# Half of the second block's modulation sums moved from the experts' down tiles into the first attention branch

## The chip, the cores and the metric

The kernel runs on one core of a Trainium2 chip. Its time is that of one execution on the device in microseconds; the time of a kernel is the median of its runs. Engines are named as the profile names them: PE is TensorE, DVE is VectorE, ACT is ScalarE, POOL is GpSimd, SP is SyncE, which here only issues transfers.

## The reference, cut to what matters

Two transformer blocks follow each other on 512 tokens of width 1024. The first block is modulated by six vectors from `silu(c) @ ada_w + ada_b`, has a mixer with two linear-attention branches (HGRN with 8 heads, then GLA with 4), and a mixture of experts (PEER). The second part (latent attention, an MLP, a state-space mixer, a second MLP) has modulation vectors of its own, made from another `c` vector in the same way:

```python
t_ctx = mixer_inputs(modulate(rmsnorm(xc, ...), mod_c[0], mod_c[1]), w_in, ...)
t_lat = mixer_inputs(modulate(rmsnorm(x, ...), mod[0], mod[1]), w_in, ...)
x = x + mod[2] * mixer_output(t_lat, context_states(t_ctx), rows, *mix_w)
x = x + mod[5] * peer(modulate(rmsnorm(x, norm_ffn_g), mod[3], mod[4]), *peer_w)
```

The second block's modulation is a product of one row of 1024 numbers with a matrix of 12288 columns. It depends on the inputs alone, so its 96 columns of 128 numbers can be made at any time before the second block begins. In the kernel one such column is one "modulation tile": 128 partitions by 1024 numbers of `w_mod`, multiplied by the row and summed along it.

## The kernel before, in words

The program is a chain of phases; each phase is one block with five instruction streams that signal each other through semaphores. Four places matter.

**The first attention branch** (`heads_phase` with `hg` true, tiles named `hgrn_...`) runs from about 57 to 494 us. Each of its 8 heads has five weight tiles (`f0`, `f1`, `q`, `v0`, `g0`; `NW` is 5), so 40 tiles of 512 KB. A tile goes through a ring of four slots (`R` is 4): SP loads it (L512) once POOL has finished the tile four places before it, ACT rounds it to its high part (L764), POOL subtracts to get its low part (L528), and PE multiplies the high and low parts. The streams walk through the iterations `it`; in one iteration PE projects head `H = it` and, between those matmuls, does the attention work of head `h = it - 1`, while the norm of head `g = it - 2` is finished. PE's order is written out by hand in `beside(g, h)`: keys, states, scores of the two directions, and then `outputs(h)` beside the `g0` product, which waits for `state_done` of both directions. DVE's order in an iteration is: `finish(g)` (L1038, L1042), `query_decay(h)` (L1010), `mask(h, 0)` (L1014), `forget(H, 0)` (L949, L950), `gates(h)` (L1033), `states(h, 0)` (L1022, L1024), `forget(H, 1)`, `differences(H, 0)` (L972 to L988: two scans and five subtractions), `mask(h, 1)`, `differences(H, 1)`, `products(H, 0)` (L1000 to L1005), `states(h, 1)`, `products(H, 1)`. `forget(H, r)` waits for ACT's store of the `f0` or `f1` product. ACT takes the exponentials of `differences` (L800 to L804) before `products` can start. In its last two iterations there is no head left to project; PE then makes the next branch's low-rank gates (`next_ranks`), which waits for `gr_lo`, the DVE instruction at L1083.

**The experts' down tiles** (`peer`, from about 1895 to 2473 us) are 128 tiles `n` of the experts' second matrix (`in_peer_v`). For each tile SP loads 512 KB of weights (L1448) and, through `load_pair`, the activations (L1633) and the gates (L1635) of the tile four places ahead. DVE multiplies activation by gate (`weigh`, L2111), makes the weights' low part (`low`, L2121) and the activations' low part (`act_low`, L2116); PE has 24 matmuls of 128x384 a tile (L1398), which wait for `p_lo` and `v_lo`. Beside them, on three tiles of four (`n % 4`), DVE makes one modulation tile (`Modulation.dot`, L192: one instruction that multiplies and sums along the row, and a short read of the sum) and one `few_add` (L2020), for which POOL fetches 128 rows of 4 KB by an indirect transfer (L1683). POOL also issues the modulation tiles' loads (L1708), each once the tile three places before is summed. One modulation tile of the 96 is left for behind the loop.

**The class `Modulation`** holds the ring of tiles, the row, and the steps: `start_act` (a sigmoid of the row on ACT, L162), `start_mul` (row times sigmoid on POOL, L166), `dot`, and `finish`, which adds the bias on POOL (L204).

**What sets the order** is the hand-written sequence on each engine; nothing is planned at run time. The expert rows and all transfers of the down tiles share the core's 16 DMA engines.

```python
for n in range(2, V_TILES):
    weigh(n)
    low(n)
    act_low(n)
    if n % 4 and m < M.tiles:
        M.dot(dve, m)
```

## Time and profile before

| what | value |
|---|---|
| median of 3 runs | 3714.02 us (3703.05 to 3714.7) |
| the profiled execution | 3709.89 us |
| its span | 3707.9 us |
| PE busy | 3422.5 us, 92% |
| DVE busy | 2415.1 us, 65% |
| ACT busy | 1508.0 us, 41% |
| POOL busy | 1163.8 us, 31% |
| first attention branch, 110 to 410 us: PE busy | 296.76 of 300 us |
| experts' down tiles, 1900 to 2460 us: PE busy | 542.54 of 560 us |

The profiled execution's own time is 2.0 us over its span. Shares of the whole span say which engine is busiest on average; which wait ends last has to be read in each stage. PE being busy means that its queue was at work, not that it ran at its peak.

### The profile page before, as it was taken

To read this page: it belongs to the slowest core of one execution; us is meant where nothing else is said; L and a number is where in the kernel's file an instruction comes from. 1 tells how busy PE (TensorE), PEld (TensorE's weight loads), DVE (VectorE), ACT (ScalarE), POOL (GpSimd) and SP (SyncE) were. 2 spreads that over 40 slices of the span, in tenths; PEclk is the share of its full clock that TensorE was granted. 3 is DMA by queue.
4 is the path that set the end of the run, shared out by engine and by line. 5 is a ranking of instruction groups with operands and counts; after the bars stand their busy time and mean duration, and the time that the engine had idled before them with its cause. 6 is when DMAs were issued, how large, how long until landed. Compare 5 with 4: busy or idle time off the path is not lost. (4 is left out here: it accounts for less than half of the span.)

```text
span 3707.9 us, 46749 instructions
## 1 busy us (share of the span) xinstructions
PE 3422.5 (92%) x17940; PEld 3005.4 (81%) x17940; DVE 2415.1 (65%) x4052; ACT 1508.0 (41%) x2046; POOL 1163.8 (31%) x797
## 2 busy tenths in 40 slices
PE   7999999979989999689979999989899998699998
PEld 6888877768889999679979999977688887678886
DVE  6655544444557999668858888876564576756354
ACT  5555555445343333345523333345442234434222
POOL 1222222127137888444432332320110024320002
PEclk9999999989999999889989999999999999899999
DMA  5111111036338889556699999961223222222331
GB/s 186 55 52 52 37 52 46 29 113 218 130 93 273 304 305 315 193 217 226 248 359 381 380 379 380 379 240 32 63 92 102 93 90 55 50 87 91 97 97 63
DMA packets 263277, 616.56 MB, mean 166 GB/s; under 512 B 93424, under 2 KB 135664, under 8 KB 260880
## 3 DMA queue, kind: packets, MB, share of 16 engines
q1 hardware_dynamic: 203968, 383.72, 31.6%
q0 software_dynamic: 55584, 202.40, 14.6%
q10 hardware_dynamic: 3504, 27.46, 1.9%
q8 instruction: 143, 2.34, 0.3%
q14 instruction: 78, 0.64, 0.0%
HBM read 556.08 MB, written 52.43 MB: 164 GB/s over the span
## 5 line engine op out<-in xcount | busy, mean ns | idle before, releaser
L1398 PE MATMUL peer_banks<-peer_h_parts,peer_w_parts 128*128 128x384 f32 (+1 forms) x3456 | 650.9, 346 | 25.7 <-POOL peer_w_parts L1688 20.4
L1398 PEld LDWEIGHTS peer_banks<-peer_h_parts,peer_w_parts 128*128 128x128 f32 x3456 | 609.4, 190 | 53.1 <-POOL peer_w_parts L1688 31.4
L1398 PE MATMUL peer_banks<-peer_act_parts,peer_w_parts 128*128 128x384 f32 x3072 | 559.9, 340 | 39.2 <-DVE peer_act_parts L2116 38.6
L1398 PEld LDWEIGHTS peer_banks<-peer_act_parts,peer_w_parts 128*128 128x128 f32 x3072 | 536.5, 190 | 60.8 <-DVE peer_w_parts L2121 43.1
L1398 PE MATMUL ffn_ps<-h_parts,ffn_w_parts 128*128 128x512 f32 x1920 | 441.4, 392 | 18.2 <-DVE h_parts L2734 11.0
L1398 PEld LDWEIGHTS ffn_ps<-h_parts,ffn_w_parts 128*128 128x128 f32 x1920 | 363.2, 189 | 95.1 <-DVE ffn_w_parts L2572 15.7
L1398 PE MATMUL ffn_ps<-ffn_hidden,ffn_w_parts 128*128 128x512 f32 x1920 | 438.1, 390 | 1.5 <-DVE ffn_hidden L2641 1.5
L1688 POOL TENSOR_TENSOR peer_w_parts<-slots,peer_w_parts 128x1024 fp32r<-128x1024 f32 x142 | 351.9, 2479 | 274.8 <-ACT peer_w_parts L1851 272.6
L1398 PEld LDWEIGHTS ffn_ps<-ffn_hidden,ffn_w_parts 128*128 128x128 f32 x1920 | 360.4, 188 | 77.7 <-issue 3.1
L1851 ACT ACTIVATE peer_w_parts<-slots 128x1024 fp32r<-128x1024 f32 x272 | 287.5, 1057 | 208.9 <-PE peer_banks L1398 191.1
L2418 ACT ACTIVATE ffn_w_parts<-slots 128x1024 fp32r<-128x1024 f32 x160 | 168.6, 1057 | 310.8 <-PE ffn_ps L1398 303.5
L2572 DVE TENSOR_TENSOR ffn_w_parts<-slots,ffn_w_parts 128x1024 fp32r<-128x1024 f32 x160 | 197.5, 1239 | 141.8 <-ACT ffn_w_parts L2418 141.5
L1398 PE MATMUL heads_proj_ps<-h_parts,hgrn_w_parts 128*128 128x512 f32 x960 | 269.1, 412 | 9.2 <-DVE hgrn_w_parts L1054 8.6
L1865 ACT ACTIVATE h<-peer_banks 128x384 f32<-128x384 f32 x128 | 63.2, 494 | 350.1 <-PE peer_banks L1398 335.5
L1398 PEld LDWEIGHTS heads_proj_ps<-h_parts,hgrn_w_parts 128*128 128x128 f32 x960 | 168.0, 190 | 39.8 <-DVE hgrn_w_parts L1054 8.7
L2385 POOL TENSOR_TENSOR ffn_total<-x 128x512 f32<-128x512 f32 x4 | 5.5, 1380 | 607.0 <-DVE x L2588 607.0
L528 POOL TENSOR_TENSOR hgrn_w_parts<-x,hgrn_w_parts 128x1024 fp32r<-128x1024 f32 x38 | 96.2, 2532 | 290.8 <-ACT hgrn_w_parts L764 290.8
L1398 PE MATMUL heads_proj_ps<-h_parts,gla_w_parts 128*128 128x512 f32 x576 | 166.3, 426 | 9.0 <-POOL gla_w_parts L528 5.1
L1683 POOL DMA_INDIRECT peer_few_rows<-in_peer_v,peer_few_idx x128 | 156.7, 1224 | 39.6 <-issue 31.3
L1708 POOL DMA_DIRECT2D peer_slab<-in_w_mod x93 | 51.9, 558 | 364.5 <-DVE peer_slab L192 352.4
L2121 DVE TENSOR_TENSOR peer_w_parts<-slots,peer_w_parts 128x1024 fp32r<-128x1024 f32 x128 | 156.1, 1220 | 11.3 <-ACT peer_w_parts L1851 11.1
L1772 PE MATMUL peer_banks<-peer_cols,h 128*128 128x128 f32 x768 | 106.9, 300 | 54.2 <-issue 40.1
(585 smaller groups left out, 5853.0 us busy)
## 6 DMA issues: line engine op xcount, KB each, us to landing
slots<-in_peer_u SPq DMA_DIRECT2D x128, 512.0 KB, 4.2
slots<-in_peer_v SPq DMA_DIRECT2D x128, 512.0 KB, 12.5
slots<-in_mlp_w SPq DMA_DIRECT2D x128, 512.0 KB, 3.5
peer_slab<-in_w_mod POOLq DMA_DIRECT2D x96, 512.0 KB, 7.2
peer_acts<-h SPq DMA_DIRECT2D x128, 192.0 KB, 5.1
peer_gates<-peer_slab ACTq DMA_DIRECT2D x16, 1536.0 KB, 13.5
peer_slab<-peer_acts SPq DMA_DIRECT2D x128, 192.0 KB, 11.8
peer_slab<-peer_gates SPq DMA_DIRECT2D x128, 192.0 KB, 11.2
```

What stands on the lines that cost most here:

```text
L528: nc.gpsimd.tensor_tensor(wp[:, m % 2, 1, :], ring[m % R], wp[:, m % 2, 0, :].bitcast(F32), ALU.subtract).then_inc(w_lo, 1)
L1398: last = nc.tensor.matmul(out, w(a, k), x(b, k), start=start and k == ks[0] and n == 0, stop=stop and k == ks[-1] and n == 2)
L1683: nc.gpsimd.indirect_dma_start(few_slot(CALLS + c), None, v_rows, bass.IndirectOffsetOnAxis(ap=few_idx[:, h, j:j + 1], axis=0)).then_inc(f ...
L1688: nc.gpsimd.tensor_tensor(wp[:, p % 2, 1, :], ring.raw[:, p % R, :], wp[:, p % 2, 0, :].bitcast(F32), ALU.subtract).then_inc(w_lo, 1)
L1708: g.dma_start(M.ring[:, i % MG, :], d["w_mod"][i + 48 + MG]).then_inc(M.ready[i % MG], 16)
L1772: last = nc.tensor.matmul(g_ps[:, b * 1024 + t * P:b * 1024 + (t + 1) * P], rows[:, b, t, :], cols[:, b, t, :], start=True, stop=True)
L1851: A(wp[:, p % 2, 0, :], ring.raw[:, p % R, :], ACT.Copy).then_inc(w_hi, 1)
L1865: A(stage[:, n % 4, :], a_ps[:, n % 2 * T:n % 2 * T + DENSE], ACT.Gelu).then_inc(gelu_done, 1)
L2121: V.tensor_tensor(wp[:, p % 2, 1, :], ring.raw[:, p % R, :], wp[:, p % 2, 0, :].bitcast(F32), ALU.subtract).then_inc(v_lo, 1)
L2385: st.then(G.tensor_tensor(total[:], K.x[:, 0, :], K.x[:, 1, :], ALU.add))
L2418: A(wp[:, m % 4, 0, :], raw[:, m % R, :], ACT.Copy).then_inc(w_hi, 1)
L2572: V.tensor_tensor(wp[:, m % 4, 1, :], raw[:, m % R, :], wp[:, m % 4, 0, :].bitcast(F32), ALU.subtract).then_inc(w_lo, 1)
```

## The change

Of the 96 modulation tiles, 48 (`MOD2_FIRST`) are now summed by DVE in the first attention branch, six in each head (`mod_dots(0)`, `mod_dots(1)`, `mod_dots(2)`, two tiles each), in the iterations that have an `h`. They use a new ring of two slots (`mod_ring`) whose second slot first holds the sigmoid. SP issues their loads: the row and tile 48 at the phase's start, tile 49 at the weight tile `m = 8`, and then `refill(i)` behind the loads of the weight tiles `f0`, `f1` and `q` of the head after next; each refill waits for two sums and issues two tiles of 512 KB. The refills of the last two heads stand at the end of SP's stream. ACT has one more sigmoid and POOL one more multiplication in the first head, and POOL adds the bias at the end. In the experts' down tiles the other 48 are summed on two tiles of four (`n % 8` of 1, 2, 3 and 5), and POOL's loop that issues their loads is written out in the order of the tiles.

```diff
@@ -437,6 +437,9 @@
     return m
 
 
+MOD2_FIRST = 48
+
+
 def heads_phase(nc, K, d, name, w_dram, heads, vt, gate_norm, y, scan_scale, lora=False, early=None, nxt=None):
 
 
@@ -459,6 +462,9 @@
         M_ = early if early is not None else heads_memory(ph, hg, vt)
         R = 4 if hg else 3
         if hg:
+            ph.sb("mod_gap", [P, 1280])
+            mod_ring = ph.sb("mod_ring", [P, 2, D])
+            MM = Modulation(nc, K, ph, d, 48, MOD2_FIRST, 2, [(2, 48)], ring=mod_ring, prod=mod_ring[:, 1:2, :])
             ring4 = K.x[:].rearrange("p (r a) t -> p r (a t)", r=R)
             ring = [ring4[:, s, :] for s in range(R)]
         else:
@@ -506,10 +512,25 @@
 
         @block.sync
         def _(sp):
+            def refill(i):
+
+                for n in (2 * i, 2 * i + 1):
+                    if n + 2 < MM.tiles:
+                        sp.wait_ge(MM.multiplied, n + 1)
+                        sp.dma_start(MM.ring[:, n % 2, :], d["w_mod"][48 + n + 2]).then_inc(MM.ready[n % 2], 16)
+
+            if hg:
+                sp.dma_start(MM.rows[:, 0, :], d["c_rows"][2].partition_broadcast(P)).then_inc(MM.rows_in, 16)
+                sp.dma_start(MM.ring[:, 0, :], d["w_mod"][48]).then_inc(MM.ready[0], 16)
             for m in range(R if hg else 2, heads * NW):
                 if m >= R:
                     sp.wait_ge(w_lo, m - R + 1)
                 sp.dma_start(ring[m % R], w_dram[m]).then_inc(ready[m % R], 16)
+                if hg and m == 8:
+                    sp.wait_ge(MM.silu, 1)
+                    sp.dma_start(MM.ring[:, 1, :], d["w_mod"][49]).then_inc(MM.ready[1], 16)
+                if hg and m >= 2 * NW and m % NW < 3:
+                    refill(3 * (m // NW - 2) + m % NW)
             if nxt is not None:
                 sp.wait_ge(nxt.zeroed, 1)
                 sp.dma_start(nxt.wgr[:].rearrange("p (k m) -> p k m", k=KT), d["w_gr"].rearrange("(k p) m -> p k m", p=P)).then_inc(nxt.gr_in, 16)
@@ -518,12 +539,16 @@
                 sp.wait_ge(h_lo, 2 * KT)
                 for m in range(2):
                     sp.dma_start(nxt.ring[:, m, :], d["w_gla"][m]).then_inc(nxt.ready[m], 16)
+                for i in range(3 * (heads - 2), 3 * heads):
+                    refill(i)
 
         @block.gpsimd
         def _(g):
             if nxt is not None:
                 nc.gpsimd.memset(nxt.gw[:], 0.0).then_inc(nxt.zeroed, 1)
             for m in range(2, heads * NW):
+                if hg and m == 6:
+                    MM.start_mul(g, nc.gpsimd)
                 g.wait_ge(w_hi, m + 1)
                 nc.gpsimd.tensor_tensor(wp[:, m % 2, 1, :], ring[m % R], wp[:, m % 2, 0, :].bitcast(F32),
                                         ALU.subtract).then_inc(w_lo, 1)
@@ -532,6 +557,7 @@
                     g.wait_ge(nxt.w_hi, m + 1)
                     nc.gpsimd.tensor_tensor(nxt.wp[:, m, 1, :], nxt.ring[:, m, :], nxt.wp[:, m, 0, :].bitcast(F32),
                                             ALU.subtract).then_inc(nxt.w_lo, 1)
+                MM.finish(g, nc.gpsimd, MM.multiplied)
 
         @block.tensor
         def _(pe):
@@ -888,6 +914,8 @@
                         gates(h)
                     if H is not None:
                         forget(H, 1)
+                        if H == 0:
+                            MM.start_act(act)
                         log_forget(H, 0)
                         log_forget(H, 1)
                         if H:
@@ -1063,11 +1091,18 @@
                         first_low(n)
                     dve.wait_ge(h_hi, n + 1)
                     V.tensor_tensor(dst[:, 1, k, :], src[:, k, :], dst[:, 0, k, :].bitcast(F32), ALU.subtract).then_inc(h_lo, 1)
+            def mod_dots(i):
+
+                for n in (6 * h + 2 * i, 6 * h + 2 * i + 1):
+                    MM.dot(dve, n)
+
             st.then(V.memset(score[:], 0.0))
             for it in range(heads + 2):
                 H = it if it < heads else None
                 h = it - 1 if 0 < it <= heads else None
                 g = it - 2 if it >= 2 else None
+                if hg and h is not None:
+                    mod_dots(0)
                 if lora and H is not None:
                     low_rank(H, 0)
                 if g is not None:
@@ -1078,6 +1113,8 @@
                     query_decay(h)
                     mask(h, 0)
                 if hg:
+                    if h is not None:
+                        mod_dots(1)
                     if h == heads - 1:
                         dve.wait_ge(nxt.gr_hi, 1)
                         V.tensor_tensor(nxt.wgp[:, 1, :], nxt.wgr[:], nxt.wgp[:, 0, :].bitcast(F32), ALU.subtract).then_inc(nxt.gr_lo, 1)
@@ -1086,6 +1123,7 @@
                     if h is not None:
                         gates(h)
                         states(h, 0)
+                        mod_dots(2)
                     if H is not None:
                         forget(H, 1)
                         differences(H, 0)
@@ -1544,7 +1582,8 @@
         gate_in_sb = flat[:, quarter // 2:quarter].rearrange("p (s b t) -> p s b t", s=4, b=TT)
         wact = flat[:, quarter:quarter + 2 * DENSE].rearrange("p (s t) -> p s t", s=2)
         MG = 3
-        M = Modulation(nc, K, ph, d, 48, 4 * 24, MG, [(2, 48)],
+        FIRST = 48 + MOD2_FIRST
+        M = Modulation(nc, K, ph, d, FIRST, 4 * 24 - MOD2_FIRST, MG, [(2, FIRST)],
                        ring=flat[:, 2 * quarter:2 * quarter + MG * D].rearrange("p (s t) -> p s t", s=MG),
                        rows=flat[:, 3 * quarter:3 * quarter + D].rearrange("p (s t) -> p s t", s=1),
                        prod=flat[:, 3 * quarter + D:3 * quarter + 2 * D].rearrange("p (s t) -> p s t", s=1))
@@ -1700,14 +1739,20 @@
             g.wait_ge(slab_out[3], 16 * TT)
             g.dma_start(M.rows[:, 0, :], d["c_rows"][2].partition_broadcast(P)).then_inc(M.rows_in, 16)
             for s in range(MG):
-                g.dma_start(M.ring[:, s, :], d["w_mod"][48 + s]).then_inc(M.ready[s], 16)
+                g.dma_start(M.ring[:, s, :], d["w_mod"][FIRST + s]).then_inc(M.ready[s], 16)
             M.start_mul(g, nc.gpsimd)
 
-            for i in range(M.tiles - MG):
-                g.wait_ge(M.multiplied, i + 1)
-                g.dma_start(M.ring[:, i % MG, :], d["w_mod"][i + 48 + MG]).then_inc(M.ready[i % MG], 16)
-                if BEFORE + LEAD + i < CALLS:
-                    fetch_down(BEFORE + LEAD + i)
+            m, c = 0, BEFORE
+            for n in range(2, V_TILES):
+                if n % 4 and m < M.tiles and n % 8 < 6:
+                    if m + MG < M.tiles:
+                        g.wait_ge(M.multiplied, m + 1)
+                        g.dma_start(M.ring[:, m % MG, :], d["w_mod"][FIRST + m + MG]).then_inc(M.ready[m % MG], 16)
+                    m += 1
+                if n % 4 and c < CALLS:
+                    if c + LEAD < CALLS:
+                        fetch_down(c + LEAD)
+                    c += 1
             M.finish(g, nc.gpsimd, M.multiplied)
             for k in (0, 2, 4):
                 g.wait_ge(sq_done, k + 2)
@@ -2131,7 +2176,7 @@
                 weigh(n)
                 low(n)
                 act_low(n)
-                if n % 4 and m < M.tiles:
+                if n % 4 and m < M.tiles and n % 8 < 6:
                     M.dot(dve, m)
                     m += 1
                 if n % 4 and c < CALLS:
```

## Rows read from the trace of the kernel before

**Rows 1.** busy times of two stretches (columns: engines, clock, DMA share, GB/s)

```profile
110.00:410.00 300.00, 296.76 (x1741) 251.98 (x1740) 163.69 (x248) 157.80 (x227) 75.50 (x30) 1.00 0.18 56
...
1900.00:2460.00 560.00, 542.54 (x2997) 521.25 (x2996) 479.96 (x653) 197.46 (x249) 167.42 (x183) 0.99 1.04 375
```

**Rows 2.** PE in order of time in the down tiles, idle before in brackets

```profile
2131.80 34.88 PE L1398 MATMUL peer_banks<-peer_act_parts,peer_w_parts 128*128 128x384 f32 x192 [0.82 <-DVE peer_act_parts L2116]
...
2259.00 56.53 PE L1398 MATMUL peer_banks<-peer_act_parts,peer_w_parts 128*128 128x384 f32 x312 [2.43 <-DVE peer_act_parts L2116]
```

**Rows 3.** waits within the down tiles: total us, times, longest

```profile
PE peer_banks L1398 <- DVE peer_act_parts L2116: 16.9, 19, 3.2
```

**Rows 4.** page, part 6: transfers, KB each, median us to landing

```profile
peer_slab<-in_w_mod POOLq DMA_DIRECT2D x96, 512.0 KB, 7.2
...
peer_slab<-peer_gates SPq DMA_DIRECT2D x128, 192.0 KB, 11.2
```

**Rows 5.** windows of 4 us around one such wait

```profile
2256.00:2260.00 4.00, 1.57 (x7) 1.28 (x6) 3.31 (x6) 1.58 (x2) 0.00 (x0) 0.87 1.06 360
2260.00:2264.00 4.00, 4.00 (x18) 4.00 (x18) 4.00 (x5) 0.53 (x1) 1.92 (x2) 0.70 1.07 362
```

**Rows 6.** one line each, durations min/median/max in ns: dot, two-input, one-input instruction

```profile
L192 DVE SCALAR_TENSOR_TENSOR peer_slab<-peer_slab x96: 1214/1219/1226, 1904.9 to 2467.1; 128x1024 f32<-128x1024 f32 x96
...
L955 DVE SCALAR_TENSOR_TENSOR gla_na<-gla_log_gate x8: 957/958/1207, 496.8 to 698.3; 128x768 f32<-128x768 f32 x8
...
L988 DVE TENSOR_SCALAR hgrn_e_kd<-hgrn_cum x16: 339/346/2487, 88.2 to 444.6; 128x256 f32<-128x256 f32 x16
```

**Rows 7.** DVE in order of time, one iteration of the first branch

```profile
208.56 0.75 DVE L1038 SCALAR_TENSOR_TENSOR hgrn_osq<-hgrn_o_ps,vec,hgrn_rstd 128x512 f32<-128x512 f32 x1 [9.54 <-ACT hgrn_rstd L836]
...
217.66 0.68 DVE L949 TENSOR_SCALAR hgrn_log_gate<-hgrn_log_gate,oml,lb 128x768 f32<-128x768 f32 x1 [5.31 <-ACT hgrn_log_gate L774]
...
225.89 0.68 DVE L949 TENSOR_SCALAR hgrn_log_gate<-hgrn_log_gate,oml,lb 128x768 f32<-128x768 f32 x1 [2.81 <-ACT hgrn_log_gate L774]
226.60 0.56 DVE L950 TENSOR_SCALAR hgrn_key<-hgrn_log_gate 128x768 f32<-128x768 f32 x1
228.92 2.13 DVE L972 TENSOR_TENSOR_SCAN hgrn_cum<-segf,hgrn_log_gate 128x512 f32<-128x512 f32 x2 [1.76 <-ACT hgrn_log_gate L785]
...
233.47 0.74 DVE L1014 COPY_PREDICATED hgrn_score<-triu,hgrn_score_ps 128x512 f32<-128x512 uint32 x1
...
235.92 2.71 DVE L980 TENSOR_TENSOR hgrn_e_k<-hgrn_cum 128x512 f32<-128x512 f32 x1
...
240.32 0.69 DVE L1000 TENSOR_TENSOR hgrn_e_k<-hgrn_e_k,hgrn_key 128x512 f32<-128x512 f32 x1
...
243.70 1.11 DVE L1024 SCALAR_TENSOR_TENSOR hgrn_state<-hgrn_state,hgrn_e_last,hgrn_kv_ps 128x128 f32<-128x128 f32 x3
```

**Rows 8.** POOL in order of time, the same iteration

```profile
218.58 2.60 POOL L528 TENSOR_TENSOR hgrn_w_parts<-x,hgrn_w_parts 128x1024 fp32r<-128x1024 f32 x1 [13.39 <-ACT hgrn_w_parts L764]
226.81 2.58 POOL L528 TENSOR_TENSOR hgrn_w_parts<-x,hgrn_w_parts 128x1024 fp32r<-128x1024 f32 x1 [5.63 <-ACT hgrn_w_parts L764]
235.46 2.62 POOL L528 TENSOR_TENSOR hgrn_w_parts<-x,hgrn_w_parts 128x1024 fp32r<-128x1024 f32 x1 [6.07 <-ACT hgrn_w_parts L764]
245.16 2.39 POOL L528 TENSOR_TENSOR hgrn_w_parts<-x,hgrn_w_parts 128x1024 fp32r<-128x1024 f32 x1 [7.07 <-ACT hgrn_w_parts L764]
```

**Rows 9.** PE, the same iteration: the first matmul of the outputs

```profile
245.12 0.39 PE L607 MATMUL hgrn_o_ps<-hgrn_score,hgrn_vtok 128*128 128x128 f32 x2
```

**Rows 10.** loads of the first branch's tiles: time to landing, and four issued together

```profile
DMA to landing us min/median/max: 3.3/3.5/6.1
...
37.78 1.75 SPq L249 DMA_DIRECT2D x<-in_w_hg  x4
```

**Rows 11.** all engines, the branch's last iteration with attention work

```profile
466.60 4.69 PE L1398 MATMUL heads_proj_ps<-h_parts,gla_wgr_parts 128*32 128x512 f32 x12 [1.27 <-DVE gla_wgr_parts L1083]
...
467.20 2.37 POOL L533 TENSOR_TENSOR gla_w_parts<-gla_ring,gla_w_parts 128x1024 fp32r<-128x1024 f32 x1 [24.32 <-ACT gla_w_parts L858]
```

## The prediction

> **What bounds the kernel now.** I read the busy times of the two stretches that the change touches first [rows 1]. In the first attention branch PE works 296.76 of 300 us and DVE 163.69: PE is the bound, and a microsecond is lost only where something makes PE wait. In the experts' down tiles PE works 542.54 of 560 us at a granted clock of 0.99, while the core's DMA engines are busy all the time (a share of 1.04) and move 375 GB/s.
>
> PE's rows in order of time show what a down tile costs [rows 2]: 192 matmuls in 34.88 us are 0.182 us each, 24 of them 4.36 us a tile, 17.4 us for four. The waits between them are 19, together 16.9 us, none longer than 3.2 [rows 3]. They end with DVE's activations, but DVE had been idle itself before them: DVE works 479.96 of 560 us, and what it waits for is the transfer that feeds `weigh`. Counting bytes says the same. Four down tiles need four weight tiles and three modulation tiles of 512 KB, three `few_add` fetches of 128 rows of 4 KB (512 KB each), and four activation and four gate slices of 192 KB [rows 4]: 6656 KB, 6.82 MB, at 375 GB/s 18.2 us, against PE's 17.4. The stage takes about 575 us for 128 tiles, 18.0 for four. So the stage is bound by transfers, by a little.
>
> A wait costs more than itself. Around the one of 2.43 us that ends at 2259.00, the granted clock is 0.87 and then 0.70 in two windows of 4 us [rows 5]: (0.13 + 0.30) x 4 = 1.7 us more.
>
> **The down tiles: what is taken away.** Half of the modulation loads go, and two of every four tiles carry one. Four tiles now move 6144 KB, 6.29 MB, 16.8 us at the same rate, under PE's 17.4. Most of the waits should go. All that there is to gain is 16.9 us of waits and about 1.7 for each of the three long ones, 22 us. A reserve of 0.6 us in four tiles is small, so I take 18; the bounds are 12 (a third of the waits, the short ones above all, stay) and 22. The 48 sums themselves, 1.22 us each by the row of the dot [rows 6], lay in DVE's idle time and give PE nothing. The one sum behind the loop goes too; the residual additions behind it are held by PE's last matmuls, so it is counted at nothing, at most 1.2 us.
>
> The Trainium skill (SBUF — State Buffer, section on rules for kernel authors) says to estimate transfers between HBM and SBUF at some 358 GB/s. This trace goes above it with 375 over 560 us. By that figure the new load of four tiles would take 17.6 us, still just over PE's 17.4, and the gain would be near 12, which is an estimate from the page and changes no term here.
>
> **The attention branch: what is added.** Each head gets six dots. A dot starts the next instruction about 1.2 us later, so a pair is 2.4 us, and DVE has room for it on average. What matters is where each pair stands, and I follow one iteration [rows 7 to 9].
>
> Pair 0 stands ahead of `finish`, where DVE idles 9.54 us. Its tiles were asked for long before. Nothing.
>
> Pair 1 follows `mask(h, 0)`, which ends near 212.3, and has until 217.66; DVE idled 5.31 us there. SP may issue its tiles once POOL has done the tile in front, 218.58 - 13.39 = 205.2. A single 512 KB load lands after 3.5 us, and the four loads issued together from 37.78 landed by 45.2 (the last one issued at 39.1, with the longest time, 6.1) [rows 10]; that is (45.2 - 37.78 - 3.3) / 3 = 1.37 for each further one, about 1.3. Behind the weight tile these two land at 210.0 and 211.3. Nothing either.
>
> Pair 2 is the trouble. It stands between `states(h, 0)`, which ends at 225.89 - 2.81 = 223.1, and `forget(H, 1)`. SP issues its tiles only when POOL has done the next weight tile, 218.58 + 2.60 = 221.2. Behind that iteration's weight load they land at 221.2 + 3.5 + 1.3 = 225.9 and 227.2. So the first dot runs from 225.9 to 227.15, when `forget` should have run.
>
> Now POOL comes in. Many DVE instructions don't run beside POOL's subtraction: L955, with two such inputs, takes 957 ns and once 1207; the one-input L988 takes 346 and once 2487 [rows 6]; and L980 at 235.92 takes 2.71 instead of 0.69, because POOL's tile began at 235.46 and ended at 238.08 [rows 7, 8]. Whoever is first is finished first. POOL asks at 226.81, during the first dot, runs from 227.15 to 229.4 (before, it ran 2.2 us after `forget` let it go), and the second dot follows it: 230.5. `forget` takes 0.71 and 0.56: 231.8. `differences(H, 0)` begins there and not at 229.39, when POOL let its scans go.
>
> The chain from there is DVE without a pause until `state_done`, and that has no slack: the last state ends at 243.70 + 1.11 = 244.81 and PE starts the outputs at 245.12 [rows 7, 9]. Without blocks, `differences(H, 0)` takes about 4.2 us (228.92 to 233.47, less what the scans waited): 236.0. But POOL's next tile asks at 235.46, when the last subtraction is just about to start (231.8 + 3.7 = 235.5). If POOL is first, that subtraction waits for POOL's end at 237.9 and the mask starts at 238.3. Before, mask to last state took 11.34 us, of which 2.02 were L980's block: 9.3 now. `products(H, 0)` stands 6.85 - 2.02 = 4.8 behind the mask, from 243.1 to 246.0, and POOL's fourth tile asks at 245.16, inside it: 2.2 more. The last state ends at 238.3 + 9.3 + 2.2 = 249.8, PE starts near 249.9 and has waited 4.8 us. A gap of that length costs clock as well; I take the 1.7 of the row [rows 5], bounds 0 and 3.4.
>
> This holds for the heads whose refills are paced by weight tiles, `h` of 0 to 5. In the first, POOL's tile comes 0.3 us earlier against the loads, and I give it the smaller stall of the next paragraph, 1.6. For `h` of 6 and 7 the refills stand at the end of SP's stream, wait only for sums and land in time. Five heads at 4.8 + 1.7 and one at 1.6 are 34.1 us.
>
> In the last iteration pair 1 stands ahead of L1083, for which PE waited already before it started the ranks at 466.60 [rows 11]. POOL asks at 467.20, between the two dots: 1.2 + 2.2 + 1.1 = 4.5 us later, all of it on PE. If POOL is not between them it is 2.4. Pair 2 lies there in idle time.
>
> The sigmoid, POOL's multiplication and SP's waits in the first head delay DVE by some 4 us between 99 and 112 us, where nothing on PE waits for it; with that cover gone they would cost those 4 once. POOL's bias addition is under 0.5 us and nobody waits.
>
> **The sum.** 34.1 + 4.5 - 18 = +20.6 us. Against the profiled execution's own 3709.9 (span 3707.9) this is 3730.5. The median shown is 4.1 above that execution and the lowest run 6.8 below it, so I put the median at 3732.
>
> **The rivals.** (a) The last subtraction gets in ahead of POOL: it starts at 235.5 and POOL asks at 235.46, so 0.1 us decides. Then mask and POOL run side by side, the scans wait for POOL (238.0), the products end before 245.16, and the last state comes at 246.6: 1.6 us a head, too short for the clock (behind a wait of 0.82 us 192 matmuls ran at the full rate [rows 2]). 6 x 1.6 + 4.5 - 18 = -3.9: 3706 by the profiled execution, 3710 by the median; not slower. For it speaks how near the two times are, against it that any delay of a landing favours POOL. (b) Between them, the subtraction is late but the products are not hit again: 2.5 and 0.5 for five heads, 15 + 1.6 + 4.5 - 18 = +3: 3717. (c) The pairs are hidden: the tiles land by 224.5, as they would if three loads took no longer than one, and the down tiles give all their 22. Then 4.5 - 22 = -17.5, with a remnant of 0.5 a head -14.5: 3697 to 3700. Against it stand the four loads of [rows 10]. (d) The change doesn't do what it says in the down tiles: the gates' landing, 11.2 us [rows 4], is set by SP's queue and not by the load, and only 6 us come back; with the forecast's stalls 3744.
>
> **How the numbers follow.** Forecast with (d) at its side 0.48, of which (d) is 0.06; (a) 0.24; (b) 0.11; (c) 0.17. About 0.3% (11 us) is what a measurement of this kernel can tell from no change. Slower by more: 0.48. Within it: (a) and (b) with a little of (c), 0.37. Faster by more: 0.15. The forecast's own range is 3724 to 3744. For eight in ten I take from 3700, which leaves out most of (c), to 3743.
>
> **What would show it.** In the changed kernel's trace: PE waits for `hgrn_state` before L607 once in each of heads 0 to 5, several us long, and the outputs of a head come some 5 us later against its `v0` product; the first dot of pair 2 follows a wait for a transfer, the second lasts 3.3 us or more; a second of L1004 or L1005 is longer than 2 us in those heads; the granted clock dips there. L1083 comes 4.5 us later against the mask ahead of it. In the down tiles PE waits fall from 19 to a few, and GB/s to about 350. The prediction is wrong if landings are quicker than 1.3 us for each further tile, if a dot does not yield to POOL, or if PE has other work ahead of the outputs.

## The result and the profile after

The changed kernel takes 3686.47 us (median of 7 runs, 3678.2 to 3696.98), the kernel before 3708.38 (7 runs beside them). The ratio is 0.9937, with a 95% interval of 0.9915 to 0.9959: faster by 0.6%, more than the 0.3% that can be told from no change. The forecast was 3732, in a range from 3700 to 3743: the result lies below the whole range, and the change made the kernel faster where slower was forecast. The span of the profiled execution falls from 3707.9 to 3684.7 us, by 23.2.

Two stretches of the changed kernel answer to [rows 1] (same columns: PE, PEld, DVE, ACT, POOL, clock, DMA share, GB/s).

```profile
110.00:410.00 300.00, 287.24 (x1681) 242.86 (x1681) 210.48 (x309) 151.13 (x216) 72.21 (x28) 1.00 0.32 113
1930.00:2430.00 500.00, 500.00 (x2883) 499.37 (x2883) 417.76 (x544) 182.93 (x241) 131.08 (x132) 1.00 1.03 362
```

The attention branch lost: PE's idle time in 300 us went from 3.24 to 12.76. The down tiles won more than I had thought there was: PE and its weight loads are busy without a gap.

PE's matmuls of the down tiles, first the line's own view (count, durations, first and last start, what ended the idle time), then one stretch in order of time and the waits inside the stage:

```profile
L1436 PE MATMUL peer_banks<-peer_act_parts,peer_w_parts x3072: 331/334/658, 1913.0 to 2450.0; 128*128 128x384 f32 x192
its engine sat idle before it (us, times) until:
  DVE peer_act_parts L2161: 21.7, 1
```

```profile
2109.72 50.60 PE L1436 MATMUL peer_banks<-peer_act_parts,peer_w_parts 128*128 128x384 f32 x291
```

The stage runs from 1913.0 to 2450.0, 537.0 us; before it ran from 1895.2 to 2472.2, 577.0. So it gives 40.0 us. The only wait is the first, ahead of the stage. But the 19 waits of [rows 3] held only 16.9 of the 40. The rest is in the matmuls: 50.60 us for 291 are 0.174 us each, where [rows 2] show 0.182, and that row has no wait inside it either. The first line above says how lateness can hide there: the record of a matmul lasts 334 ns, but the next one starts 174 ns behind it. One that starts up to 0.16 us late still begins inside the record ahead of it and leaves no idle time. In the trace of the kernel before, five of the seven tiles that follow the first in that row of 192 begin 0.32 to 0.35 us behind the last matmul of the tile ahead, instead of 0.17.

The branch gives back 17.8 of them, since the stage begins that much later. The outputs of the heads (PE, first matmul of a head, idle before it in brackets) show where:

```profile
146.11 0.46 PE L633 MATMUL hgrn_o_ps<-hgrn_score,hgrn_vtok 128*128 128x128 f32 x2 [1.29 <-issue]
...
199.91 0.46 PE L633 MATMUL hgrn_o_ps<-hgrn_score,hgrn_vtok 128*128 128x128 f32 x2 [2.34 <-issue]
...
253.62 0.46 PE L633 MATMUL hgrn_o_ps<-hgrn_score,hgrn_vtok 128*128 128x128 f32 x2 [2.25 <-issue]
...
306.48 0.46 PE L633 MATMUL hgrn_o_ps<-hgrn_score,hgrn_vtok 128*128 128x128 f32 x2 [1.37 <-issue]
```

Before, they began at 142.60, 193.91 and 245.12 (the last in [rows 9]), one every 51.2 us. Now the first is 3.5 us late and each of the next five heads adds 2.2 on average (2.6, 2.5, 1.7, 2.6 and 1.6): the seventh head's outputs begin at 464.39 instead of 449.92, 14.5 late. Behind them come the ranks, [rows 11]; here PE and POOL, and the two dots on DVE between which POOL got in:

```profile
485.54 4.18 PE L1436 MATMUL heads_proj_ps<-h_parts,gla_wgr_parts 128*32 128x512 f32 x12 [5.69 <-DVE gla_wgr_parts L1120]
```

```profile
481.71 2.34 POOL L558 TENSOR_TENSOR gla_w_parts<-gla_ring,gla_w_parts 128x1024 fp32r<-128x1024 f32 x1 [24.42 <-ACT gla_w_parts L884]
```

```profile
480.60 1.21 DVE L192 SCALAR_TENSOR_TENSOR hgrn_mod_ring<-hgrn_mod_ring,hgrn_c_rows 128x1024 f32<-128x1024 f32 x1
...
481.74 3.40 DVE L192 SCALAR_TENSOR_TENSOR hgrn_mod_ring<-hgrn_mod_ring,hgrn_c_rows 128x1024 f32<-128x1024 f32 x1
...
485.07 0.41 DVE L1120 TENSOR_TENSOR gla_wgr_parts<-gla_wgr,gla_wgr_parts 128x256 fp32r<-128x256 f32 x1
```

The wait rose from 1.27 to 5.69, by 4.4; the ranks are 18.9 late. The sum is 14.5 + 4.4 - 40.0, with 1.1 won between the ranks and the down tiles and 1.0 behind them: -23.2, the difference of the spans. The 1.1 is less than executions differ by: the kernel before, `half_loads` and `half_sums` (below) have the same code up to the down tiles and reach them at 1895.2, 1894.8 and 1891.4.

### The profile page after: what moved, and what is told of

Same layout as the page of the kernel before. It is cut to its first block and busy times, and to the rows that moved or that the text cites. A ratio compares the mean times of both kernels' runs of the same rounds, so it can differ in the third digit from the quotient of the medians.

```text
span 3684.7 us, 46757 instructions
## 1 busy us (share of the span) xinstructions
PE 3401.0 (92%) x17940; PEld 3002.9 (81%) x17940; DVE 2434.0 (66%) x4052; ACT 1500.3 (41%) x2047; POOL 1131.0 (31%) x751
## 3 DMA queue, kind: packets, MB, share of 16 engines
q8 instruction: 143, 2.34, 0.3%
## 5 line engine op out<-in xcount | busy, mean ns | idle before, releaser
L1436 PE MATMUL peer_banks<-peer_act_parts,peer_w_parts 128*128 128x384 f32 x3072 | 537.3, 336 | 21.7 <-DVE peer_act_parts L2161 21.7
L1436 PE MATMUL ffn_ps<-h_parts,ffn_w_parts 128*128 128x512 f32 x1920 | 442.0, 393 | 18.2 <-DVE h_parts L2779 10.9
L1722 POOL DMA_INDIRECT peer_few_rows<-in_peer_v,peer_few_idx x128 | 148.2, 1158 | 126.5 <-DVE peer_few_acc L2065 97.4
L1817 PEld LDWEIGHTS peer_banks<-peer_cols,h 128*128 128x128 f32 x768 | 102.2, 211 | 58.6 <-issue 58.6
```

The lines of the kernel that those rows point to most:

```text
L1436: last = nc.tensor.matmul(out, w(a, k), x(b, k), start=start and k == ks[0] and n == 0, stop=stop and k == ks[-1] and n == 2)
L1722: nc.gpsimd.indirect_dma_start(few_slot(CALLS + c), None, v_rows, bass.IndirectOffsetOnAxis(ap=few_idx[:, h, j:j + 1], axis=0)).then_inc(f ...
L1817: last = nc.tensor.matmul(g_ps[:, b * 1024 + t * P:b * 1024 + (t + 1) * P], rows[:, b, t, :], cols[:, b, t, :], start=True, stop=True)
```

## The experiments

### What sets the pace of the down tiles

**Each half of the change alone.** `branch_only` has the 48 sums in the branch and still all 96 beside the down tiles, so 48 are made twice:

```diff
-        FIRST = 48 + MOD2_FIRST
-        M = Modulation(nc, K, ph, d, FIRST, 4 * 24 - MOD2_FIRST, MG, [(2, FIRST)],
+        FIRST = 48
+        M = Modulation(nc, K, ph, d, FIRST, 4 * 24, MG, [(2, FIRST)],
...
-                if n % 4 and m < M.tiles and n % 8 < 6:
+                if n % 4 and m < M.tiles:
```

> The changed kernel's 48 sums in the attention branch stay, and the down tiles again do all 96 as before (the first 48 are made twice). Theory of two separate shares: the branch costs its 18.9 us up to the ranks, the down tiles take their 576.6 us again, so about +18 us against before. Rival, that the two halves act on each other (the branch's cost is only seen because of something later): under +8.

Measured: 3725.52 us, ratio 1.0045 (1.0026 to 1.0064). The down tiles run from 1914.5 to 2488.0, 573.5 us. When nothing pays for it the branch costs 17 us by the ratio and 14 by the medians, near the 18 expected and well above the rival's 8.

`down_only` leaves the 48 sums of the branch out, with their loads, the sigmoid and the multiplication (their columns are zero), and has the other 48 on two tiles of four. Of its edits to the changed kernel:

```diff
             def mod_dots(i):
-                for n in (6 * h + 2 * i, 6 * h + 2 * i + 1):
-                    MM.dot(dve, n)
+                return
...
-                MM.finish(g, nc.gpsimd, MM.multiplied)
+                nc.gpsimd.memset(K.mod[:, 48:96], 0.0)
```

> Nothing of the change in the attention branch (its 48 columns are set to zero and never summed); the down tiles as in the changed kernel. Theory of two separate shares: -40 us against before, with the first down matmul at 1895 and PE at 4.16 us a tile. My forecast's step (PE needs 4.36 us a tile, only the waits can go): -18 to -22.

Measured: 3672.81 us, ratio 0.9896 (0.9879 to 0.9912); the stage runs from 1899.2 to 2435.7, 536.5 us. So the gain of 40 us belongs to the down tiles, and the loss to the branch.

**Transfers or VectorE.** Taking a sum away takes two things away, 512 KB of transfer and 1.22 us of DVE. Both kernels here are the kernel before with one of the two halved. `half_loads` makes all 96 sums, every second one over the data that already lie in the ring:

```diff
-                g.dma_start(M.ring[:, i % MG, :], d["w_mod"][i + 48 + MG]).then_inc(M.ready[i % MG], 16)
+                if (i + MG) % 2 == 0:
+                    g.dma_start(M.ring[:, i % MG, :], d["w_mod"][i + 48 + MG]).then_inc(M.ready[i % MG], 16)
```

> The kernel before with all 96 sums in the down tiles, but only every second modulation tile is loaded; the others are summed over what lies in the slot, so their values are not the modulation's. It takes away the transfers and leaves DVE its work. Theory T (transfers set the pace of the down tiles): nearly all of the 40 us come back, stage about 540. Theory V (DVE sets it: its five instructions of a tile with a sum take 4.42 us back to back, against 4.16 of PE): three tiles of four stay at 4.42, the stage stays at 560 or more, gain under 16.

`half_sums` loads all 96 tiles and replaces every second sum by a memset of its one column:

```diff
-                    M.dot(dve, m)
+                    (M.skip if m % 2 else M.dot)(dve, m)
```

> The kernel before with all 96 loads in the down tiles, but every second sum is left out (a one-column memset stands in its place and releases the slot), so half of the second block's modulation is missing. It takes away DVE's work and leaves the transfers. Theory T: 6.82 MB in four tiles at 380 GB/s are 17.9 us, the stage stays near 575 and nothing is gained. Theory V: the stage falls to about 540, -35 us.

Measured: `half_loads` 3668.76 us, ratio 0.9888 (0.9869 to 0.9907), stage 1894.8 to 2431.2, 536.4 us. `half_sums` 3705.6, ratio 0.9987 (0.9977 to 0.9996), stage 1891.4 to 2464.9, 573.5 us. The same stretch of both, `half_loads` first:

```profile
1930.00:2430.00 500.00, 500.00 (x2892) 500.00 (x2890) 463.03 (x634) 189.13 (x244) 153.68 (x130) 1.00 1.01 354
```

```profile
1930.00:2430.00 500.00, 475.66 (x2673) 468.31 (x2672) 386.08 (x544) 172.66 (x222) 153.88 (x168) 0.99 1.05 380
```

With DVE busier than in the kernel before (463 of 500 us, 431 before) and half the modulation loads, PE never starves; with DVE at 386 and all loads, it starves as before. The transfers set the pace, and DVE does not. `half_loads` also frees POOL from issuing half of the loads; that it is the bytes that count rests on the DMA share of 1.05 and on the byte counts below, not on a run of its own.

**How many have to go.** `moved_32` takes the third pair out of each head and leaves 64 sums beside the down tiles, on four of every eight; `moved_16` keeps only the pair at the start of an iteration and leaves 80, on five of every eight. Their edits to the changed kernel, that of `moved_32` first:

```diff
-MOD2_FIRST = 48
+MOD2_FIRST = 32
...
-                if hg and m >= 2 * NW and m % NW < 3:
-                    refill(3 * (m // NW - 2) + m % NW)
+                if hg and m >= 2 * NW and m % NW < 2:
+                    refill(2 * (m // NW - 2) + m % NW)
...
-                for n in (6 * h + 2 * i, 6 * h + 2 * i + 1):
+                for n in (4 * h + 2 * i, 4 * h + 2 * i + 1):
...
-                        mod_dots(2)
...
-                if n % 4 and m < M.tiles and n % 8 < 6:
+                if n % 4 and m < M.tiles and (n % 8 < 6 or n == 6):
```

```diff
-MOD2_FIRST = 48
+MOD2_FIRST = 16
...
-                if hg and m >= 2 * NW and m % NW < 3:
-                    refill(3 * (m // NW - 2) + m % NW)
+                if hg and m >= 2 * NW and m % NW == 0:
+                    refill(m // NW - 2)
...
-                if n % 4 and m < M.tiles and n % 8 < 6:
+                if n % 4 and m < M.tiles and (n % 8 < 7 or n == 7):
```

> 32 sums in the branch, two pairs a head and no third pair; 64 beside the down tiles, on four of every eight tiles as the 48 are in the changed kernel, but up to the stage's end. Theory T (transfers set the pace of the down tiles until their rate is low enough for PE to): the changed kernel's stage moves 355 GB/s x 520 us and 16 tiles more come to 8.4 MB, so 199 MB in the whole stage, which at the 380 GB/s of the kernel before takes 524 us, less than PE's 532: the stage stays at 537 to 541 us. The branch costs 8 to 10 us instead of 18.9. Time about 3677 to 3681. Rival (each sum beside the down tiles costs its share, 40 us / 48 = 0.83 us, whatever the rate): the stage takes 550, and the time is 3690.

> 16 sums in the branch, only the pair at the start of each iteration; 80 beside the down tiles, on five of every eight tiles. Theory T (the down tiles take the longer of PE's time and the bytes at some 380 GB/s): 199 MB of the kernel with 32 moved and 16 tiles more of 0.52 MB are 208 MB, at 380 GB/s 547 us, above PE's 532, so the stage takes 547 to 552 us; the first output is within 2 us of the kernel before, the ranks too; the time about 3681 to 3686, 10 us above the kernel with 32. Rival (even spreading of the sums over the tiles is what counted, or every sum costs its share of 0.83 us): the stage takes 537 to 541 with even spreading and the time 3671, or 564 and the time 3697.

Measured: `moved_32` 3674.1 us, ratio 0.9905 (0.9883 to 0.9926), stage 539.2 us (1897.9 to 2437.1), as the byte count said. In the changed kernel the sums beside the down tiles are used up early (the last begins at 2318.5, and the stage's last quarter carries none); `moved_32` fills that quarter, and the stage grows by only 2.2 us. `moved_16` 3690.55, ratio 0.9955 (0.9939 to 0.9972), stage 555.8 us (1899.3 to 2455.1): above the forecast of 547 to 552 (and of 3681 to 3686 for the time), and below the rival's 564. Its stretch and its waits:

```profile
1930.00:2430.00 500.00, 493.83 (x2773) 478.22 (x2772) 429.41 (x578) 180.88 (x231) 152.88 (x158) 1.00 1.05 379
```

```profile
PE peer_banks L1433 <- DVE peer_act_parts L2158: 27.1, 9, 21.7
```

Of its 27.1 us of waits 21.7 are the first, ahead of the stage, so 5.4 us lie inside, and yet the stage is 18.8 us longer than with 48 moved. Counting bytes gives the rest. Eight down tiles need 10240 KB without modulation and 512 KB for each modulation tile. At the 380 GB/s at which the engines are full (share 1.05) six, five and four tiles per eight make 35.9, 34.5 and 33.1 us, and PE needs 537.0 / 16 = 33.6. The longer of the two, times 16: 574, 552 and 537, against 577.0, 555.8 and 537.0 to 539.2 measured. PE's 33.6 is itself taken from the measured 537.0, so the independent figures are 574 and 552. So the last step of 16 tiles back to 96 costs 21.2 us, 1.33 each, close to the 1.38 us that 512 KB take at that rate; the step from 64 to 48 is worth 2.2 at most.

The Trainium skill (HBM Reference, Specifications) says that a core that streams alone goes well above its share of some 358 GB/s. The trace agrees in that, with 380 GB/s over 500 us; the some 425 that the page gives as measured are not reached here.

### What the branch costs, and why less than forecast

One iteration of the changed kernel, DVE in order of time, is the counterpart of [rows 7]; POOL's rows are those of its subtraction of [rows 8]:

```profile
232.12 1.23 DVE L192 SCALAR_TENSOR_TENSOR hgrn_mod_ring<-hgrn_mod_ring,hgrn_c_rows 128x1024 f32<-128x1024 f32 x1 [3.00 <-DMA hgrn_mod_ring<-in_w_mod]
...
233.38 3.29 DVE L192 SCALAR_TENSOR_TENSOR hgrn_mod_ring<-hgrn_mod_ring,hgrn_c_rows 128x1024 f32<-128x1024 f32 x1
...
241.50 2.55 DVE L1016 TENSOR_SCALAR hgrn_e_kd<-hgrn_cum 128x256 f32<-128x256 f32 x1
...
251.17 0.69 DVE L1033 TENSOR_TENSOR hgrn_e_q<-hgrn_e_q,hgrn_q 128x512 f32<-128x512 f32 x1
...
252.41 1.11 DVE L1052 SCALAR_TENSOR_TENSOR hgrn_state<-hgrn_state,hgrn_e_last,hgrn_kv_ps 128x128 f32<-128x128 f32 x3
```

```profile
232.84 2.74 POOL L553 TENSOR_TENSOR hgrn_w_parts<-x,hgrn_w_parts 128x1024 fp32r<-128x1024 f32 x1 [5.63 <-ACT hgrn_w_parts L790]
241.51 2.39 POOL L553 TENSOR_TENSOR hgrn_w_parts<-x,hgrn_w_parts 128x1024 fp32r<-128x1024 f32 x1 [5.92 <-ACT hgrn_w_parts L790]
251.25 2.83 POOL L553 TENSOR_TENSOR hgrn_w_parts<-x,hgrn_w_parts 128x1024 fp32r<-128x1024 f32 x1 [7.35 <-ACT hgrn_w_parts L790]
```

In this iteration the chain is the one that was forecast up to the mask: the wait for the third pair's transfer, the second dot lengthened beside POOL (3.29), the last subtraction lengthened too (2.55 for 0.35). The products are not: L1033 takes its usual 0.69, and the states end 2.7 us later in the iteration than before, not 5.

In the next head the subtraction is not caught. It begins 0.04 us ahead of POOL, where above it was 0.01:

```profile
295.20 0.35 DVE L1016 TENSOR_SCALAR hgrn_e_kd<-hgrn_cum 128x256 f32<-128x256 f32 x1
```

```profile
295.24 2.56 POOL L553 TENSOR_TENSOR hgrn_w_parts<-x,hgrn_w_parts 128x1024 fp32r<-128x1024 f32 x1 [5.94 <-ACT hgrn_w_parts L790]
```

That is rival (a) of the prediction. Of the six heads with the late transfer, the second, third and fifth are caught and add 2.5 to 2.6 us; the fourth and sixth are not and add 1.6 to 1.7; the first is not either. In `branch_only`, whose branch is the same, four of the six are caught, and not the same ones.

**Is that luck?** L1033 began 0.08 us ahead of POOL's fourth tile. `late_memset` puts a short memset in front:

```diff
                         mod_dots(2)
+                        if H is not None:
+                            nc.vector.memset(gap[:, 0:256], 0.0)
```

> The changed kernel with a memset of 128x256 elements on VectorE, some 0.3 us, behind the third pair in seven heads: no loads, no sums. In the changed kernel the last product of the head ends at 251.86 and POOL's fourth subtraction begins at 251.25, and the products were not lengthened: by my chain they escaped it by less than 0.1 us. Theory E (a knife edge): 0.3 us later the last product is caught and lasts 2.5 us or more, the states' end moves by 2 us a head or more and the time rises by 12 us or more. Rival (the order of the two engines keeps the product clear): the outputs come 0.3 us later each, and the time rises by 2 us.

Measured: 3693.48 us (10 runs, 3686.54 to 3707.75), ratio 0.9966 (0.9953 to 0.9979). The memset takes 0.27 us. The same iteration:

```profile
251.50 0.68 DVE L1033 TENSOR_TENSOR hgrn_e_q<-hgrn_e_q,hgrn_q 128x512 f32<-128x512 f32 x1
```

```profile
251.56 2.85 POOL L553 TENSOR_TENSOR hgrn_w_parts<-x,hgrn_w_parts 128x1024 fp32r<-128x1024 f32 x1 [7.33 <-ACT hgrn_w_parts L790]
```

None of the 12 L1033 between 142 and 455 us was lengthened (mean 681 ns; 684 in the changed kernel). But the memset does not test the edge at the products. This iteration is 0.30 us late before its memset begins (the third pair's first dot is at 232.42, in the changed kernel at 232.12), and the memset's own 0.27 us are absorbed by the last subtraction, which again waits for POOL:

```profile
241.89 2.48 DVE L1016 TENSOR_SCALAR hgrn_e_kd<-hgrn_cum 128x256 f32<-128x256 f32 x1
```

```profile
241.81 2.42 POOL L553 TENSOR_TENSOR hgrn_w_parts<-x,hgrn_w_parts 128x1024 fp32r<-128x1024 f32 x1 [5.93 <-ACT hgrn_w_parts L790]
```

From the end of POOL's third tile on, the two kernels run alike: L1033 begins 7.3 us behind that end, and POOL's fourth tile 9.7 us behind the third's start. POOL's requests do not follow DVE's chain. They come behind ACT's rounding (L790), which stands in ACT's order behind its store of PE's product, and the store had waited for PE (the changed kernel, fourth tile):

```profile
249.36 0.38 ACT L797 ACTIVATE hgrn_v<-heads_proj_ps 128x256 f32<-128x256 f32 x1 [2.81 <-PE heads_proj_ps L1436]
...
250.11 1.06 ACT L790 ACTIVATE hgrn_w_parts<-x 128x1024 fp32r<-128x1024 f32 x1
```

So they keep their place against PE: the fourth tile begins 0.12 us ahead of the moment at which PE starts to wait for the outputs (251.25 against 253.62 - 2.25 = 251.37), and before it began 0.04 us behind the outputs' start [rows 8, 9]. In the 12 heads of the changed kernel, `branch_only` and `late_memset` whose subtraction was caught, L1033 is listed between 0.08 us ahead of POOL's fourth tile and 0.01 behind it, and it took its 0.68 to 0.69 us each time. So it was luck, of a kind that repeats: the products escape by less than 0.1 us in each such head. What they would take 0.2 us later was not tried.

More heads are caught at the subtraction here. L1016 averages 938 ns over 11 in the changed kernel and 1128 here, which with 0.35 and 2.5 us for the two cases is 3 of 11 caught and 4 of 11:

```profile
L1016 DVE TENSOR_SCALAR hgrn_e_kd<-hgrn_cum 128x256 f32<-128x256 f32 x11 | 10.3, 938 | 0.0
```

```profile
L1016 DVE TENSOR_SCALAR hgrn_e_kd<-hgrn_cum 128x256 f32<-128x256 f32 x11 | 12.4, 1128 | 0.0
```

The first head, outside that stretch, is caught here too, so it is three heads against five. The seventh head's outputs begin at 468.19, 3.8 later. Two more caught heads are 1.9 of them, and 1.7 are clock: behind the fifth head's wait of 2.33 us the granted clock was 0.58 from 362 to 366 us, where the changed kernel has 1.00. That leaves some 0.2 us for all seven memsets. The medians differ by 7 us, but they were taken at different times, the runs of both kernels scatter over 19 to 21 us, and the two profiled spans are equal (3684.8 and 3684.7); what the memset costs in all stays open. That the caught heads and the dips of the clock also make these runs scatter, where the four of `early_refill_ranks` (below) lie within 0.9 us, is likely but not shown, since one execution of each kernel is profiled.

**The transfer of the third pair.** `early_refill` asks for it one weight tile earlier, and for the next head's first pair too, which had time either way:

```diff
-                if hg and m >= 2 * NW and m % NW < 3:
-                    refill(3 * (m // NW - 2) + m % NW)
+                if hg and m >= 2 * NW and m % NW < 2:
+                    i = 3 * (m // NW - 2)
+                    for r in ((i, i + 1), (i + 2,))[m % NW]:
+                        refill(r)
```

> The changed kernel with the third pair's loads asked for one weight tile earlier in every head (behind the first tile of the head instead of the second); sums, their places and the down tiles are as they are. Theory B (the branch's loss is the third pair: it waits 3.00 us for its transfer and pushes the states, whose end the outputs wait for): the wait of about 3 us before L192 is gone, the outputs' waits of 1.3 to 2.3 us in heads 2 to 7 are gone, the ranks' matmuls begin near 475 instead of 485.5, and the time falls by about 10 us to 3676. Rival (the second dot of the third pair is caught by another of POOL's subtractions, or the earlier transfers slow the weight tiles): the waits move and stay, and the time falls by 3 us or less.

Measured: 3679.4 us, ratio 0.9912 (0.9891 to 0.9932). The dots of all heads together, in the changed kernel and here (sum, mean ns | idle before and what ended it):

```profile
L192 DVE SCALAR_TENSOR_TENSOR hgrn_mod_ring<-hgrn_mod_ring,hgrn_c_rows 128x1024 f32<-128x1024 f32 x48 | 71.8, 1523 | 20.9 <-DMA hgrn_mod_ring<-in_w_mod 19.4 <-DVE hgrn_e_q L1033 1.3
```

```profile
L192 DVE SCALAR_TENSOR_TENSOR hgrn_mod_ring<-hgrn_mod_ring,hgrn_c_rows 128x1024 f32<-128x1024 f32 x48 | 56.8, 1219 | 2.7 <-DMA hgrn_mod_ring<-in_w_mod 1.4 <-DVE hgrn_e_q L1035 1.3
```

The waits for transfers fall from 19.4 to 1.4 us and no dot is lengthened any more. The outputs of the first seven heads begin every 51.2 us again, with no wait before them, the seventh at 451.71, and the ranks begin at 472.82. The third head's:

```profile
246.92 0.39 PE L635 MATMUL hgrn_o_ps<-hgrn_score,hgrn_vtok 128*128 128x128 f32 x2
```

So the late transfer, with the subtractions that it let collide, was the branch's loss in the middle heads: 12.7 of the 14.5 us. The 7 us between the medians are less than that: the down tiles begin at 1905.6, 7.4 us earlier than in the changed kernel. Most of the 5.3 us in between went in clock. Over the 60 us around the ranks the granted clock is 0.80 here (450 to 510 us) and 0.86 in the changed kernel (460 to 520), which is 3.6 us, and 5.2 are gone by the first matmul of the mixer's output product (815.3 against 822.8).

**The last head.** In two kernels the last head's second pair stands behind the low-rank subtraction:

```diff
-                    if h is not None:
+                    if h is not None and h < heads - 1:
                         mod_dots(1)
                     if h == heads - 1:
                         dve.wait_ge(nxt.gr_hi, 1)
...
+                        mod_dots(1)
```

> As the kernel with 32 moved sums, and in the last head the second pair of sums stands behind the low-rank subtraction instead of ahead of it. If the 4.5 us of the tail are that subtraction made late by the pair (a dot lengthened to 3.40 us by POOL, and the other), the wait of 5.69 us before the ranks' matmuls falls back to about 1.3 and the time falls by another 4 to 4.5 us, to 3673 to 3677. Rival: something else behind it is as late, and the time falls by 1 us or less.

> 48 moved, loads asked for earlier as in the kernel with early refills, and in the last head the second pair behind the low-rank subtraction. The wait of 4.67 us before the ranks' matmuls falls to about 1, the ranks begin near 469, the time falls by some 4 us against early refills alone, to about 3675: the same as the kernel with 32 moved and this order (3672), since both stages of down tiles are at PE's pace. Rival (the pair, moved behind, makes the third pair and the forget gate late, and the last head's outputs with them): the last outputs stay at 491 and the time at 3679.

Measured: `moved_32_ranks` 3672.17 us, ratio 0.9899 (0.9883 to 0.9916), ranks at 467.71; from `moved_32` (470.36, a wait of only 2.08) there was less to win than I had written, and the time fell by 2 us. `early_refill_ranks` 3671.01 us (3670.58 to 3671.49), ratio 0.9902 (0.9886 to 0.9919), ranks with no wait at all:

```profile
468.11 3.76 PE L1439 MATMUL heads_proj_ps<-h_parts,gla_wgr_parts 128*32 128x512 f32 x12
```

Against `early_refill` the time fell by 8 us where some 4 were forecast, more than the wait of 4.67 that is gone: the granted clock from 450 to 510 us is back at 0.89, as in the kernel before, from 0.80. The last outputs begin at 485.15 against 484.56 before: the 48 sums now cost the branch 0.6 us there, and 1.5 at the ranks. Every run of both is below the lowest of the changed kernel (3678.2), and they stand where `down_only` stands, which makes no sums in the branch at all; which of the two is better can't be told.

## Why the prediction was wrong

Two terms of the sum failed, and it took both to leave the range.

**The first step that failed: "All that there is to gain is 16.9 us of waits and about 1.7 for each of the three long ones, 22 us."** The stage gave 40.0, and the sum with 40 in the place of 18 is -1.4, on the other side. I had taken PE's 4.36 us a tile [rows 2] for its floor, because the row shows no wait. But a start that comes up to 0.16 us late leaves no idle time in the row, since each record lasts 334 ns; and the ends of matmuls in this profile are modelled, so that some that are fed late are shown as longer ones (the mean from 1900 to 2460 us is 339 ns, in the changed kernel from 1930 to 2430 it is 334). PE's own pace is 4.19 us a tile (537.0 / 128), 0.175 us a matmul. The transfers' 18.2 us for four tiles, which I had also worked out, should have been set against 16.8 and not 17.4: 1.2 us (by the 18.0 that the stage took) to 1.4 for each four tiles, times 32, is 38 to 45.

The kernel before had the number. In [rows 1] the weight loads (PEld) are busy 521.25 us for 2996, which is 0.174 each, the fed pace, and they leave 38.75 of the 560 us idle, where the matmuls leave 17.46. The reading is rough: in 500 us of `half_sums` they leave 31.7 and in `moved_16` 21.8, for stages that are 36.5 and 18.8 us longer than the fed one. The Trainium skill (Perfetto Trace Analysis, Identifying the Most-Contended Engine) says that the busy share of matmuls is a bad measure of how near TensorE is to its limit and names that of the weight loads instead (beside MFU, the work done as a share of the peak). The traces agree: PEld goes to 499.37 of 500 us in the changed kernel.

**The bound: right.** Transfers set the pace of the stage, by experiment: 536.4 us with half of the modulation loads and 573.5 with half of the sums. That it is "by a little" was wrong in size. Rival (d), gates that land late for SP's sake, fell: the waits for them did not hold the stage once the loads were gone.

**The second step that failed, in the branch: 34.1 us for 14.5, right in kind and more than twice too large.** The first two pairs cost nothing and the third waited for its transfer, 3.00 us. POOL collided with the second dot (3.29 us) in all six heads, as forecast. But "POOL's fourth tile asks at 245.16, inside it: 2.2 more" failed in every head. POOL did ask inside the products, at 251.25 in an iteration that PE reached 6.0 us later than before; the product then at work was the last of the five, had begun 0.08 us earlier, and was finished first. And the collision with the last subtraction, on which "0.1 us decides", came in some heads and not in others, where I had let it come in all five. The caught heads added 2.5 to 2.6 us, rival (b)'s 2.5; the others of the five 1.6 to 1.7, rival (a)'s 1.6. The first head cost 3.5 us and not 1.6, of which 1.29 is its wait before the outputs.

The clock term of 1.7 a head has the right size and the wrong count. In the changed kernel the granted clock stayed at 1.00 through all these waits. In `branch_only`, with the same branch, it fell behind two of the six, those of 2.27 us before 252.93 and of 2.26 us before 414.86:

```profile
252.00:256.00 4.00, 3.07 (x18) 3.01 (x19) 3.93 (x8) 0.74 (x2) 1.38 (x1) 0.77 0.37 102
256.00:260.00 4.00, 4.00 (x24) 3.63 (x23) 2.46 (x5) 0.00 (x0) 0.00 (x0) 0.81 0.09 33
...
411.00:415.00 4.00, 1.74 (x9) 1.15 (x8) 3.67 (x9) 3.68 (x6) 2.52 (x1) 0.95 0.00 0
415.00:419.00 4.00, 4.00 (x20) 3.87 (x21) 3.85 (x6) 0.00 (x0) 0.31 (x1) 0.63 0.65 171
```

Each is (0.23 + 0.19) x 4 or (0.05 + 0.37) x 4, 1.7 us.

**The tail, 4.5 us: right.** 4.4, with POOL between the two dots, of which the second took 3.40 us.

**The signs that I named.** Waits before the outputs, the dot of 3.3 us, the ranks' delay and the missing waits in the down tiles are all in the trace. A second product over 2 us and a dip of the clock are not. GB/s fell to 362, not to 350.

**The sum again.** From +20.6 to -23.2 are 43.8 us: 22.0 of the down tiles, 19.6 of the branch, 0.1 of the tail, and 2.1 outside the three terms. With the branch and the tail as measured and the gain as forecast the sum would be 14.5 + 4.4 - 18 = +0.9, 3712; with the gain as measured and the rest as forecast it is -1.4, 3710. Both lie inside the range. The forecast's median stands 1.5 us above its sum and the rivals' times about 4 above theirs, a difference that changes nothing here.

## What to carry to other kernels

A row of matmuls without waits does not show TensorE's floor: compare the mean of one, or the weight loads' busy time, with a stretch that is certainly fed, before you cap a gain at the waits. Where two resources are within some per cent of each other, count the bytes and the matmuls' time of one period for both and take the longer; with the rate and PE's pace read from two of these traces that gave each stage length here within 1%. When work is put into an engine's idle time, look first at when its data land: asking for one pair of tiles a step earlier took 12.7 us off the branch and 7 off the time, and one pair moved in the last head another 8. Where two engines meet within 0.1 us, one profile shows one outcome; price both, and expect other executions to differ.

## What the runs showed of the hardware

The core's transfers ran at 379 to 380 GB/s over 500 us, with a DMA share of 1.05, in the four kernels whose down tiles they bound (the kernel before, `branch_only`, `half_sums`, `moved_16`). At 378 GB/s PE was still fully fed with four modulation tiles in eight (the changed kernel):

```profile
2000.00:2100.00 100.00, 100.00 (x578) 99.80 (x577) 86.38 (x114) 36.92 (x49) 29.11 (x30) 1.00 1.06 378
```

A wait's cost in clock depends on more than its length: a wait of 2.43 us in the down tiles of the kernel before was followed by a clock of 0.70 [rows 5], one of 2.27 us in the branch of `branch_only` by 0.77 and 0.81, and the changed kernel's waits of 2.25 to 2.34 us at the same place by none below 1.00. A dot of two SBUF inputs takes 1.22 us alone and 3.29 to 3.40 beside POOL's subtraction. The Trainium skill (SBUF — State Buffer, Who interferes with whom) says that in such a pair the one that starts second is blocked until the first is done, and the trace agrees for L1033, which began 0.08 us ahead of POOL and kept its 0.69 us. The dot of 3.29 us is listed 0.54 us behind POOL's start and ends 1.1 us, about a dot's own time, behind POOL's end.
